# A decoder step on one core: copies of the sample caches moved from the state update to the down projection

## Chip, cores and metric

One core of one Trainium2 chip runs the whole kernel in one launch. The metric is the device time of that launch in microseconds (us).

## What is computed

The reference runs one layer of a hybrid decoder on a prompt of 512 tokens and on 8 sample tokens (one token for each of 8 sequences), width 1024, everything in float32. What matters here:

```python
# GLA, sample side: a state S of 4 heads x 128 x 256 per sequence (0.5 MB) is read, updated and written back
S = S * exp(blast) + k^T v ;  o = q @ S
# sliding-window attention, sample side: three caches per sequence (128, 512 and 1024 positions of 1024 floats);
# the new caches are the old ones shifted by one position, with the new key and value at the end
new_buf = stack([kall, vall])[:, kall.shape[1] - Lb:]
# attention scores get a relative bias looked up by distance; then branch projections, the output projection,
# and a gated FFN:
y = (silu(a_conv) * b) @ w_down
x = x + gate2 * y_f ;  out = rmsnorm(x)
```

The shift of a cache is nothing but a copy from DRAM to DRAM of all positions but the first: 508 KB for each of the 8 caches of group 1, 2044 KB for each of the 8 of group 2, and 4092 KB for each of the 8 of group 3. Nothing in the kernel reads these copies.

## The kernel before, in words

**Tiling.** The 520 token columns (512 + 8) stand on the free axis in two halves of 260, the features on the partitions. Every large matrix product is done in three passes (high part times high part, low part of the activations, low part of the weights), so a block of 128 x 128 weights costs six matmuls (`three_pass`, line 361). Weights come in units of 1 MB (`stream`), each unit being two output tiles of 8 blocks; a unit goes through three steps: SP's queue loads it into one of two slots of `wraw` (`issue`, `load`, line 318), ScalarE rounds it into `whi` (`split_hi`, line 332), VectorE subtracts to get `wlo` (`split_lo`, line 345). A slot of `wraw` is free for the next load once VectorE has finished its split.

**Stages.** In program order: an opening with the modulation vectors and the first norm; the GLA input units; the stage "gla" (11 units: the projections of attention group 0 and some gates are multiplied while the GLA recurrence runs between them); "att0" (9 units), "att1" (6) and "att2" (4), in which the attention of one group runs between the units of the next; the branch and output projections; the FFN's up projection (a loop over 22 units); and the down projection (8 output tiles `m`, each of two halves of 11 blocks with a load of 704 KB each). Then comes the final norm and the store of y.

**Order inside a streamed stage.** `stream_pe`, `stream_act` and `stream_dve` walk the stage's units. A `Between` object spreads the steps of the side work (generators such as `gla_pe`, `attention_pe`) evenly over four places in each unit. So each engine has one fixed order in which pieces of the unit's matmuls and steps of the side work alternate, and a side step that waits holds up the unit's matmuls behind it.

**The side work of "gla".** It has 41 steps over the 44 places of its 11 units: four heads of the prompt's recurrence, then two steps of preparation, then the 8 sample states (from about 0.75 of the stage on), then two steps that finish. For each sample state GpSimd's queue loads the state (line 1047) and a copy of the sample's value row broadcast over 128 partitions (line 1049), 512 KB each, into a ring of four slots; ScalarE scales the values by k (line 936), VectorE updates the state (line 1011), TensorE reads it out with q (line 883), and GpSimd stores it (line 1057, 512 KB). The first four loads are issued together. After that GpSimd waits, for each load, until the store of the state that was in the slot has landed and has been read out.

**The side work at the start of "att0".** GpSimd loads the table `onehot` (line 1160), VectorE waits for it (line 1196), TensorE makes the bias by distance (lines 1173 and 1175), VectorE evacuates it (line 1201), GpSimd writes it to DRAM (line 1162) and reads it back in a skewed form into `hank` (three DMAs, line 1167), and TensorE flips it (line 1185). SP's queue stores the GLA output, 2080 KB (line 1503), in the same stretch.

**The cache copies.** `moves` is a list of 33 copies in a fixed order: the small `conv_s` one, 8 of group 1 (508 KB), 8 of group 2 (2044 KB), 16 of group 3 (half a cache each, 2046 KB). Each call of `move_cache` (line 287) issues the next one on ScalarE's queue. `stream_act` calls it at the start of each of the 30 units of the four streamed stages, and the down projection calls it before each `split_hi`, 16 calls of which only the first three still find a copy. ScalarE waits for all copies at the very end, after its last instruction for y.

Of the kernel before, what the change touches and what calls it, by code (L numbers as in the profile page):

```python
# [139 lines left out]
def program(nc, w, o, con):  # L140
    U = stream(w)
# [22 lines left out]
    with ctx:  # L164
# [67 lines left out]
        def s(name):  # L232

            if name not in S:
                S[name] = sem(name)
            return S[name]
# [37 lines left out]
        for g in range(NG):  # L274
            pieces = 2 if g == 2 else 1
            for b in range(NS):
# [3 lines left out]
                for i in range(pieces):  # L280
                    r = slice(P // pieces * i, P // pieces * (i + 1))
                    moves.append((dst[r], src[r]))
        n_moved = [0]

        def move_cache(act):
            if n_moved[0] < len(moves):
                act.dma_start(*moves[n_moved[0]]).then_inc(caches_moved, 16)
                n_moved[0] += 1
# [161 lines left out]

        def stream_act(act, us, dst, work, steps, fine=False):
            between = Between(work, steps, us, fine)
            for u in us:
                move_cache(act)
                copy_tiles(act, u, dst, U[u]["m0"], between)
            between.finish()

# [80 lines left out]
        def square_act(act, i, k, X, tmp):  # L538
            if k >= 2:
                act.wait_ge(s("sq_added"), (KD - 1) * i + max(1, k - 2))  # L540
            act.activation(tmp["sq"][:, k % 2, :], X[:, k, :], ACT.Square).then_inc(s("sq_ready"), 1)
# [208 lines left out]
        def phase(name):  # L750
            return [u for u, x in enumerate(U) if x.get("phase") == name]
# [741 lines left out]
        for g in range(NG - 1):  # L1493
            with nc.Block() as block:
                us, here, there = phase(f"att{g}"), AQKV[g], AQKV[1 - g]
# [191 lines left out]
        with nc.Block() as block:  # L1687
            g_last = NG - 1
            us, here = phase("att2"), AQKV[g_last % 2]
# [45 lines left out]
            @block.scalar  # L1735
            def _(act):
                stream_act(act, us, None, attention_act(act, g_last, join_act(act)), n_steps, fine=True)
# [214 lines left out]
        with nc.Block() as block:  # L1952
# [36 lines left out]
            def _(act):  # L1989
# [22 lines left out]
                        unit(i, d, False)  # L2012
                for m in range(KD):
                    for half in range(2):
                        move_cache(act)
                        split_hi(act, vd0 + 2 * m + half + 1)
                    if m >= 1:
                        act.wait_ge(s("x_new"), KD + m)
                        if m == 1:
                            act.wait_ge(s("stored0"), CONV0 + 32 * (KF // 2))  # L2020
                            act.wait_ge(s("stored1"), CONV0 + 32 * (KF // 2))
                        square_act(act, 2, m - 1, xT, n3)
# [265 lines left out]
```

## Time and profile before

| | us |
|---|---|
| median of 3 runs | 1387.3 (1383.27 to 1394.7) |
| the profiled execution, its own time | 1388.96 |
| its span, first to last instruction | 1387.3 |
| mean granted TensorE clock in it | 0.945 of full speed |

Outside the span lie 1.7 us of the profiled execution. TensorE is busy for 91% of the span. A granted clock of 1.00 is 2.4 GHz, one of 0.50 is 1.2 GHz, and a number between them over a stretch is a mean of the two. TensorE's busy time in a stretch can therefore be high while it does half the work. Queue 0 in the DMA rows is GpSimd's, queue 1 is SP's, queue 10 is ScalarE's, that is the cache copies'.

### The profile page before, as it was taken

How to read it: one execution, taken by the hardware profiler on the slowest of the kernel's cores; microseconds unless marked ns; L12 is line 12 of the kernel's file. 1: busy time of each engine (PE TensorE's matmuls, PEld its weight loads, DVE VectorE, ACT ScalarE, POOL GpSimd, SP SyncE). 2: the span in 40 equal slices, each digit the busy share in tenths (PEclk: the TensorE clock that was granted, in tenths of full speed). 3: DMA queues.
4: the chain of work that ended last, by engine and by line, in shares of the span. 5: the costliest groups of instructions: out<-in, count | busy, mean ns of one | idle time of the engine just before them, and what ended most of it. 6: DMA issues, size and time to landing. Idle time of an engine off the chain costs nothing. (4 is left out here: it accounts for less than half of the span.)

```text
span 1387.3 us, 23268 instructions
## 1 busy us (share of the span) xinstructions
PE 1256.2 (91%) x9753; PEld 1159.8 (84%) x9753; DVE 611.1 (44%) x958; ACT 484.8 (35%) x770; POOL 107.0 (8%) x193
## 2 busy tenths in 40 slices
PE   5599999999679999999988689997899999999997
PEld 3479998888567998888776568997799999999996
DVE  0633134445331334343444836555766565652332
ACT  1573233344342443244242215333533333321212
POOL 1000000001211000020122011100000000010000
PEclk9589999999898999999989779999899999999998
DMA  7635543233986746666655647843333333346221
GB/s 230 198 122 173 162 127 103 88 110 122 369 321 247 245 152 224 217 229 218 224 183 199 245 139 267 283 152 91 92 92 91 90 90 89 86 131 198 84 83 61
DMA packets 165377, 229.84 MB, mean 166 GB/s; under 512 B 7316, under 2 KB 147982, under 8 KB 163868
## 3 DMA queue, kind: packets, MB, share of 16 engines
q1 hardware_dynamic: 148532, 123.76, 28.8%
q10 hardware_dynamic: 1424, 54.52, 10.8%
q0 software_dynamic: 15344, 50.45, 10.5%
q8 instruction: 59, 0.97, 0.3%
q14 instruction: 18, 0.15, 0.0%
HBM read 202.96 MB, written 80.26 MB: 204 GB/s over the span
## 5 line engine op out<-in xcount | busy, mean ns | idle before, releaser
L361 PE MATMUL ps<-actH,whi 128*128 128x260 f32 x2064 | 449.0, 300 | 25.0 <-DVE actL L573 17.8
L361 PE MATMUL ps<-actL,whi 128*128 128x260 f32 x2064 | 425.8, 289 | 0.0
L361 PE MATMUL ps<-actH,wlo 128*128 128x260 f32 x2064 | 425.4, 289 | 0.0
L361 PEld LDWEIGHTS ps<-actH,whi 128*128 128x128 f32 x2064 | 328.9, 196 | 68.1 <-issue 54.9
L361 PEld LDWEIGHTS ps<-actL,whi 128*128 128x128 f32 x2064 | 329.4, 195 | 0.0
L361 PEld LDWEIGHTS ps<-actH,wlo 128*128 128x128 f32 x2064 | 328.3, 195 | 0.0
L345 DVE TENSOR_TENSOR wlo<-wraw,whi 128x512 fp32r<-128x512 f32 (+3 forms) x95 | 141.1, 1498 | 188.5 <-ACT whi L332 187.8
L332 ACT ACTIVATE whi<-wraw 128x512 fp32r<-128x512 f32 (+3 forms) x95 | 119.6, 1275 | 135.9 <-PE ps L361 80.7
L410 ACT ACTIVATE arena<-ps 128x520 f32<-128x520 f32 x76 | 45.4, 600 | 219.3 <-PE ps L361 219.2
L361 PE MATMUL ps<-gH,whi 128*128 128x260 f32 x352 | 71.7, 285 | 0.0
L361 PE MATMUL ps<-gH,wlo 128*128 128x260 f32 x352 | 71.5, 285 | 0.0
L361 PE MATMUL ps<-gL,whi 128*128 128x260 f32 x352 | 71.4, 285 | 0.0
L1399 ACT ACTIVATE arena<-arena 128x128 f32<-128x128 f32 (+1 forms) x96 | 39.9, 417 | 54.0 <-DVE arena L1376 54.0
L2050 DVE TENSOR_TENSOR wlo<-wraw,whi 128x2048 fp32r<-128x2048 f32 x22 | 50.4, 2293 | 18.0 <-ACT whi L1995 18.0
L361 PEld LDWEIGHTS ps<-gL,whi 128*128 128x128 f32 x352 | 54.9, 190 | 0.0
L361 PEld LDWEIGHTS ps<-gH,wlo 128*128 128x128 f32 x352 | 54.9, 191 | 0.0
L361 PEld LDWEIGHTS ps<-gH,whi 128*128 128x128 f32 x352 | 54.8, 190 | 0.0
L515 DVE COPY arena<-ps 128x256 f32<-128x256 f32 x24 | 10.1, 422 | 77.8 <-PE ps L496 77.8
L1995 ACT ACTIVATE whi<-wraw 128x2048 fp32r<-128x2048 f32 x22 | 41.8, 1901 | 0.0
L1370 DVE SCALAR_TENSOR_TENSOR arena<-ps,arena 128x512 f32<-128x512 f32 (+1 forms) x32 | 20.9, 653 | 39.7 <-PE ps L1321 39.7
L496 PE MATMUL ps<-wraw,scP 128*32 128x256 f32 x384 | 31.1, 451 | 5.7 <-DMA wraw<-in_w_ada 5.7
L1977 POOL DMA_DIRECT2D out_conv_p<-arena x22 | 11.3, 514 | 323.5 <-DVE arena L2091 217.9
(306 smaller groups left out, 1456.7 us busy)
## 6 DMA issues: line engine op xcount, KB each, us to landing
wraw<-in_w_in SPq DMA_DIRECT2D x38, 1024.0 KB, 5.4
out_win_s<-in_cache_win ACTq DMA_DIRECT2D x16, 2046.0 KB
wraw<-in_w_ada SPq DMA_DIRECT2D x24, 1024.0 KB, 5.5
wraw<-in_w_up SPq DMA_DIRECT2D x44, 512.0 KB, 5.0
out_win_s<-in_cache_win ACTq DMA_DIRECT2D x8, 2044.0 KB
raw_gates<-arena SPq DMA_DIRECT2D x24, 260.0 KB, 6.0
arena<-raw_gates POOLq DMA_DIRECT2D x24, 260.0 KB, 4.5
wraw<-in_w_down SPq DMA_DIRECT2D x16, 384.0 KB, 3.3
```

The source lines that it names most:

```text
L332: ins = act.activation(whi[:, v % 2, c], wraw[:, u % 2, c], ACT.Copy)
L345: ins = dve.tensor_tensor(wlo[:, v % 2, c], wraw[:, u % 2, c], whi[:, v % 2, c].bitcast(F32), ALU.subtract)
L361: last = pe.matmul(ps[:, 2 * (n % 2) + a, 0:HT], wt, X[:, k0 + j, a * HT:a * HT + HT], start=begin and j == 0 and wt is hi and X is H, sto ...
L410: act.activation(halves(to), banks(n), ACT.Copy).then_inc(tile_read["act"], 1)
L496: last = pe.matmul(ps[QC * j:QC * j + QC, 7, 0:2 * P], scP[:, k, :], wraw[:, u % 2, 2 * k * P:2 * (k + 1) * P], start=half == 0, stop=half ...
L515: dve.tensor_copy(rows[:, a % 2, :], ps[:, 7, 0:2 * P]).then_inc(ada_tok, 1)
L1370: dve.scalar_tensor_tensor(sv, ps[:, 4 + n % 2, 0:nh * J].rearrange("p (h k) -> p h k", k=J), SCALE, biasT[:, hs, lo:hi], ALU.mult, ALU.ad ...
L1399: last = act.activation(sv, sv, ACT.Exp, bias=bnd[:, c % 2, b0 + AE:b0 + AE + 1], accum_out=bnd[:, c % 2, b0 + AE + 1:b0 + AE + 2])
L1977: pool.dma_start(o["conv_p"][:, col], ast[0:2, store.slot, :]).then_inc(s(f"stored{store.slot}"), 16)
L1995: act.activation(whi[:, vn % 2, :], wraw[:, (up0 + 1 + d) % 2, :], ACT.Copy).then_inc(hi_ready, 1)
L2050: dve.tensor_tensor(wlo[:, vn % 2, :], wraw[:, (up0 + 1 + d) % 2, :], whi[:, vn % 2, :].bitcast(F32), ALU.subtract).then_inc(lo_ready, 1)
```

## The change

`stream_act` calls `move_cache` only in the first six of the eleven units of the stage "gla" (`M_GLA = 6`); in the other stages it calls it in every unit, as before. The down projection calls it once for each output tile `m` instead of twice. The order of the list stays as it is, so every later copy moves back by five calls:

| stage | copies before | copies after |
|---|---|---|
| gla | conv, 8 of group 1, 2 of group 2 | conv, 5 of group 1 |
| att0 | 6 of group 2, 3 of group 3 | 3 of group 1, 6 of group 2 |
| att1 | 6 of group 3 | 2 of group 2, 4 of group 3 |
| att2 | 4 of group 3 | 4 of group 3 |
| down projection | 3 of group 3 | 8 of group 3 |

```diff
@@ -281,6 +281,7 @@
         n_moved = [0]
+        M_GLA = 6
 
         def move_cache(act):
@@ -450,8 +451,9 @@
             between = Between(work, steps, us, fine)
-            for u in us:
-                move_cache(act)
+            for j, u in enumerate(us):
+                if U[u]["phase"] != "gla" or j < M_GLA:
+                    move_cache(act)
                 copy_tiles(act, u, dst, U[u]["m0"], between)
             between.finish()
@@ -2012,7 +2014,8 @@
                 for m in range(KD):
                     for half in range(2):
-                        move_cache(act)
+                        if half == 0:
+                            move_cache(act)
                         split_hi(act, vd0 + 2 * m + half + 1)
```

## Rows read from the trace of the kernel before

**Rows 1.** The page: TensorE's busy time; queue 10, packets, MB, share.
```profile
PE 1256.2 (91%) x9753; PEld 1159.8 (84%) x9753; DVE 611.1 (44%) x958; ACT 484.8 (35%) x770; POOL 107.0 (8%) x193
...
q10 hardware_dynamic: 1424, 54.52, 10.8%
```

**Rows 2.** DMA issues of the whole span: the small copies.
```profile
out_win_s<-in_cache_win ACTq DMA_DIRECT2D x8, 508.0 KB
```

**Rows 3.** Busy time in stretches of 5 us, 370 to 440 us.
```profile
core 0: us, PE busy (x) PEld busy (x) DVE busy (x) ACT busy (x) POOL busy (x), PEclk, DMA share, GB/s
...
370.00:375.00 5.00, 0.99 (x9) 0.78 (x7) 0.00 (x0) 0.00 (x0) 2.04 (x3) 1.00 1.01 360
...
380.00:385.00 5.00, 5.00 (x26) 4.80 (x23) 1.67 (x4) 1.71 (x4) 1.93 (x4) 0.50 0.99 362
...
415.00:420.00 5.00, 5.00 (x16) 2.23 (x17) 2.19 (x4) 0.00 (x0) 0.60 (x1) 0.60 1.03 435
420.00:425.00 5.00, 5.00 (x34) 5.00 (x33) 0.00 (x0) 0.60 (x1) 2.71 (x3) 0.72 0.28 68
...
435.00:440.00 5.00, 3.54 (x11) 2.51 (x12) 0.00 (x0) 0.60 (x1) 0.00 (x0) 0.66 0.81 284
```

**Rows 4.** Groups of instructions by line, 345 to 405 us.
```profile
L883 PE MATMUL ps<-arena 128*32 128x256 f32 x64 | 5.6, 425 | 12.5 <-DVE arena L1011 12.5
```

**Rows 5.** DMA queues, 345 to 405 us: packets, MB, share.
```profile
q0 software_dynamic: 3456, 12.58, 57.8%
q10 hardware_dynamic: 96, 4.19, 19.1%
```

**Rows 6.** Timeline of ScalarE: start, us, what, [idle before it].
```profile
359.40 0.52 ACTq L287 DMA_DIRECT2D out_win_s<-in_cache_win  x1
...
375.73 1.70 ACT L936 ACTIVATE arena<-arena 128x256 f32<-128x256 f32 x4 [8.10 <-DMA arena<-sample_values]
...
403.86 0.53 ACTq L287 DMA_DIRECT2D out_win_s<-in_cache_win  x1
...
427.41 0.52 ACTq L287 DMA_DIRECT2D out_win_s<-in_cache_win  x1
```

**Rows 7.** Timeline of GpSimd, 364 to 405 us.
```profile
364.72 0.76 POOL L1047 DMA_DIRECT2D arena<-in_state_gla  x1 [4.50 <-DMA out_gla_s<-arena]
...
404.89 0.55 POOL L1160 DMA_DIRECT2D arena<-in_onehot  x1
```

**Rows 8.** Timeline of TensorE, 379 to 415 us.
```profile
379.19 1.08 PE L883 MATMUL ps<-arena 128*32 128x256 f32 x8 [8.20 <-DVE arena L1011]
...
414.19 0.80 PE L1173 MATMUL ps<-arena 33*8 33x384 f32 x2 [3.26 <-DVE arena L1196]
```

**Rows 9.** Who waited for whom, 404 to 440 us.
```profile
PE ps L1185 <- DMA arena<-bias_by_distance: 2.9, 1, 2.9
```

**Rows 10.** DMA issues, 1240 to 1265 us: KB, median to landing.
```profile
out_win_s<-in_cache_win ACTq DMA_DIRECT2D x3, 2046.0 KB
...
wraw<-in_w_down SPq DMA_DIRECT2D x2, 320.0 KB, 15.1
```

**Rows 11.** Timeline of ScalarE in the down projection.
```profile
1263.66 1.38 ACT L332 ACTIVATE whi<-wraw 128x1408 fp32r<-128x1408 f32 x1 [10.83 <-DMA wraw<-in_w_down]
...
1299.00 1.38 ACT L332 ACTIVATE whi<-wraw 128x1408 fp32r<-128x1408 f32 x1 [6.53 <-PE ps L361]
...
1347.85 0.62 ACT L541 ACTIVATE arena<-arena 128x520 f32<-128x520 f32 x1
```

**Rows 12.** Timeline of VectorE in the down projection.
```profile
1284.56 1.63 DVE L345 TENSOR_TENSOR wlo<-wraw,whi 128x1408 fp32r<-128x1408 f32 x1 [6.18 <-ACT whi L332]
```

**Rows 13.** Timeline of the loads' and outputs' queue (SP), 1243 us on.
```profile
1243.81 99.72 SPq L318 DMA_DIRECT2D wraw<-in_w_down  x26
...
1382.91 1.04 SPq L1969 DMA_DIRECT2D out_y_sample<-arena  x1
```

**Rows 14.** The chain that ended last: start, us, what.
```profile
1241.80 128.46 PE ps L361 x1056
```

## The prediction

> **What bounds the kernel now.** I read the page's busy times first: TensorE is busy for 91% of the span, no other engine for half of it [rows 1]. So time is only to be won where TensorE idles or runs at its lower clock, and the question is whether a copy stands behind such a place. The busy time in stretches of 5 us shows where those places are: between 370 and 375 us TensorE works for 0.99 us, and from 380 to 385 us it is "busy" for all 5 us with a granted clock of 0.50, the lower level, so it does half the work; the same pair, a gap and then a lower clock, stands around 410 to 425 us and around 435 us [rows 3]. The groups of instructions say that in the sample states TensorE idled 12.5 us before the read-outs (line 883) [rows 4], and the timeline that 8.20 us of it are one wait, for the fifth state [rows 8]. ScalarE began that state at 375.73 after 8.10 us of waiting for a DMA, the broadcast value row [rows 6]. Then I looked at what the DMA engines did there.
>
> **What a copy costs the others.** ScalarE's queue kept 16 engines busy for 10.8% of 1387.3 us, which is 149.8 us, for 54.52 MB [rows 1]: 2.75 us a MB. A copy of 2046 KB (2.10 MB) is 5.8 us of all engines, one of 508 KB (0.52 MB) [rows 2] is 1.4 us. In the sample states queue 0 moved 12.58 MB in 3456 packets, 3.6 KB each, and the copies 4.19 MB in 96, 44 KB each; together with SP's queue they filled the engines [rows 5], with a DMA share of 0.99 and 1.01 [rows 3]. A copy of this kind, once started, is thus a block that small packets of another queue stand behind.
>
> **Term 1, the sample states.** Five copies leave the stage: three of 508 KB, before the states are loaded, where nothing waits for a DMA (I count them at nothing), and two of 2044 KB. The first of these two was issued at 359.40 [rows 6], while GpSimd waited 4.50 us for a store to land, so that it could issue the fifth load at 364.72 [rows 7]. That load landed 11 us later (375.73), against the 5.8 us by which the copy fits in between. Without the copy the load comes at least 5.8 us sooner, and the store before it a little sooner as well. What is late then: TensorE reaches the read-out at 379.19 - 8.20 = 371.0 and would still wait one or two us, and the later states go by the pace of their own DMAs, 12.58 MB at 57.8% of the engines. So the whole is pulled forward by the shift of the DMAs, not by all that TensorE lost. Bounds: 0 (the states' own 12.6 MB set the pace in any case) and 8.2 + 2.5 = 10.7 (the whole gap, and (1 - 0.50) x 5 us of lower clock). I take 6.5. The second copy, at the end of the states, has no wait of TensorE's behind it: 0.
>
> **Term 2, the table of the bias.** The first copy of "att0" was issued at 403.86 [rows 6], the table `onehot` at 404.89 [rows 7]; TensorE waited 3.26 us for what VectorE makes of it, until 414.19 [rows 8]. That copy becomes one of 508 KB, 4.4 us shorter, so the table lands 4.4 us sooner and the gap of 3.3 us goes; next is TensorE itself. The lower clock behind the gap cost (1 - 0.60) x 5 + (1 - 0.72) x 5 = 3.4 us [rows 3]. Part of that stretch is small matmuls which wait for each other through VectorE, so I count on two thirds of it. Bounds 0 and 6.7; I take 3.3 + 2.2 = 5.5.
>
> At this place a rule of the Trainium skill speaks against the change. The page "DMA: Bandwidth & Descriptors", section "Issuing engines are not separate DMA queues", says that DMAs from different engines run on the same 16 DMA engines and interleave. If they shared evenly, the table's 0.2 MB would have landed early in spite of the copy, its wait would have another cause, and term 2 would be 0, the sum 9.5. The packet sizes of rows 5 speak for the block instead.
>
> **Term 3, the flipped bias.** The second copy of "att0" (427.41) [rows 6] ran into the three loads of the skewed bias, and TensorE waited 2.9 us for them [rows 9], with (1 - 0.66) x 5 = 1.7 us of lower clock after it [rows 3]. This copy too shrinks by 4.4 us. But TensorE now comes to the place sooner, by the 2.2 us of clock of term 2, so 2.9 - 4.4 + 2.2 = 0.7 us of the wait stay. Gain 2.2, and 0.8 of the clock: 3.0. Bounds 0 and 4.6. The third copy shrinks too, and nothing waits there: 0. From the fourth unit of "att0" to the end of "att2" every call issues about the same 2.1 MB as before: 0.
>
> **Term 4, the down projection.** It gets eight copies in place of three. TensorE's chain runs through it without a break: 128.46 us for 16 halves, 8.03 us each [rows 14]. What a half's weights may cost: VectorE ends a split at 1284.56 + 1.63 = 1286.2 [rows 12], then SP loads the half that ScalarE rounds at 1299.00 [rows 11], 12.8 us later. The two splits take 1.38 and 1.63 us and TensorE needs the result a half after 1299.00, so 8.0 - 3.0 = 5 us are left over: a load may take 17.8 us. In the first tile, where three copies stood in 12 us, one load took from 1243.81 [rows 13] to 1263.66, 19.8 us, and ScalarE waited 10.83 us for it [rows 11], and even then TensorE's chain is one piece [rows 14]. The median of the two 320 KB loads there was 15.1 us [rows 10]. With one copy per tile (16 us) a load has at most 5.8 us in front of it. So the stage costs 0, between 0 and 25 (below); a gain is excluded, since nothing there waits now. The issue itself, 0.52 us on ScalarE [rows 6], lies in idle time of over 6 us [rows 11]. The last copy is issued behind the square at 1347.85 [rows 11], about 34 us before the last output's DMA at 1382.91 [rows 13]; it needs 5.8. Cost at the end: 0.
>
> **Sum.** 6.5 + 5.5 + 3.0 = 15.0 us. The profiled execution took 1388.96 us, so 1374.0 after. The median of the runs is 1.7 us lower, and the forecast goes by it: 1387.3 - 15.0 = 1372.3, said as 1372.
>
> **Rivals.** (a) *Only part of it.* The states' own DMAs fill the engines, so the time saved on the copy is waited for again at the next state, and only the two waits in "att0" go: 5.5 + 3.0 = 8.5 us, 1379; or the reverse, term 1 alone with 6.5, 1381. For it: DMA share near 1.0 even in 370 to 375 us, where no copy ran [rows 3]. Against it: a load that took 11 us with 5.8 us of copy in it. Chance 0.27, at 1380. (b) *All waits and their lower clock go*: 10.7 + 6.7 + 4.6 = 22 us, 1365. For it: each low clock stands behind a gap. Chance 0.15. (c) *Slower.* The down projection's loads come too late behind their copies. It decides at 17.8 us from issue to landing. At the 19.8 us seen once, 2.0 us would be missing in each of seven tiles, and a gap of that size brings some 1.5 us of lower clock (the 8.2 us gap brought over 2.5): 7 x 3.5 = 25 us. With the three terms gained this is 1397, without them 1412. Against it: it takes a load to stand behind two or more copies, and there is one in 16 us. Chance 0.05. (d) *The copies were hidden and nothing moves*: other DMAs take the same room; 1387. Chance 0.03.
>
> **How the numbers follow.** The forecast holds 0.50, with 1368 to 1376 as its own range (11 to 19 us). A measurement of this kernel can tell some 1% from no change, which is 13.9 us, or 1373.4. Two thirds of the forecast's range lie below that. Faster by over 1%: 0.50 x 0.66 + 0.15 = 0.48. Within 1%: 0.17 + 0.27 + 0.03, and half of (c) with 0.02, so 0.49. Slower by over 1%: the rest of (c), 0.03. The range, 1364 to 1384, takes in (a), (b) and the forecast, and leaves out (c), (d) and the outer ends.
>
> **What would show it.** In the changed profile: the wait of TensorE before the read-outs falls from 12.5 to about 6 us; ScalarE's longest wait for the value row from 8.1 to under 3; `onehot` lands in under 6 us from its issue, and no wait stands before line 1173; the wait before line 1185 is under 1 us; granted clocks near 1.00 where 0.50, 0.60, 0.72 and 0.66 stood; queue 10 absent between the sixth unit of "gla" and "att0"; the down projection's chain again 128 to 129 us, with eight copies beside it and ScalarE waiting for no load. The forecast is wrong if the sample states last as long as before with queue 10 silent, if new waits for a DMA stand in "att0", or if the down projection's chain is cut.

## The result, and the profile after

The changed kernel took 1380.3 us (median of 20 runs, 1374.84 to 1388.68), the kernel before, on the same chip, 1391.5 us (20 runs, 1382.77 to 1395.83). The ratio is 0.9937, interval 0.9919 to 0.9954: 0.6% faster, some 8.8 us. The forecast had 15.0 us, 1.1%. The direction was right; the gain is little more than half of it. Measured a second time, beside 35 runs of the kernel before, the ratio was 0.9959 (0.9930 to 0.9989), 5.7 us. The two intervals reach from 6.4 to 11.3 us and from 1.5 to 9.7 us.

The profiled execution took 1376.58 us (span 1374.9), 12.4 us less than the one of before. Not all of that is the change's: the opening, up to ScalarE's first pass over the norm, took 59.8 us in the one and 55.8 in the other, although nothing is changed there, and over all the profiles of this study, changed or not, it took 54.4 to 60.8. These 4.0 us are scatter. The stretch from the middle of "att2" to the down projection scatters too, 472.5 and 472.0 us before and 470.5 and 472.0 after in two profiles each, and I compare pieces of the span from here on.

Lines of the changed kernel stand one to three further down: L883 is L885, L936 is L938, L1173 is L1175, L1185 is L1187, L361 is L362.

The page of the kernel after: TensorE is busy 9.0 us less, and queue 10 has the same packets and megabytes as in [rows 1]. Nothing was saved, only moved.
```profile
PE 1247.2 (91%) x9753; PEld 1152.7 (84%) x9753; DVE 611.2 (44%) x958; ACT 484.9 (35%) x770; POOL 107.4 (8%) x193
...
q10 hardware_dynamic: 1424, 54.52, 11.0%
```

The sample states after. First the timeline of ScalarE at the eight states (start, us, what, [idle before it]), the rows that answer to the second one of [rows 6]:
```profile
346.15 1.70 ACT L938 ACTIVATE arena<-arena 128x256 f32<-128x256 f32 x4 [2.06 <-DMA arena<-sample_values]
352.02 1.71 ACT L938 ACTIVATE arena<-arena 128x256 f32<-128x256 f32 x4 [4.16 <-DMA arena<-sample_values]
356.71 1.70 ACT L938 ACTIVATE arena<-arena 128x256 f32<-128x256 f32 x4
360.12 1.69 ACT L938 ACTIVATE arena<-arena 128x256 f32<-128x256 f32 x4
366.14 1.71 ACT L938 ACTIVATE arena<-arena 128x256 f32<-128x256 f32 x4 [1.62 <-DMA arena<-sample_values]
372.12 1.71 ACT L938 ACTIVATE arena<-arena 128x256 f32<-128x256 f32 x4 [4.27 <-DMA arena<-sample_values]
377.96 1.70 ACT L938 ACTIVATE arena<-arena 128x256 f32<-128x256 f32 x4 [3.64 <-DMA arena<-sample_values]
```
And the same timeline of the kernel before: its first state, and its fourth to eighth without the fifth, which stands in [rows 6] (375.73, 8.10 us of waiting).
```profile
350.54 1.71 ACT L936 ACTIVATE arena<-arena 128x256 f32<-128x256 f32 x4 [1.00 <-DMA arena<-sample_values]
...
363.23 1.70 ACT L936 ACTIVATE arena<-arena 128x256 f32<-128x256 f32 x4
...
380.84 1.71 ACT L936 ACTIVATE arena<-arena 128x256 f32<-128x256 f32 x4 [3.41 <-DMA arena<-sample_values]
386.13 1.70 ACT L936 ACTIVATE arena<-arena 128x256 f32<-128x256 f32 x4
390.81 1.71 ACT L936 ACTIVATE arena<-arena 128x256 f32<-128x256 f32 x4 [1.18 <-DMA arena<-sample_values]
```
The fifth state comes 6.0 us after the fourth instead of 12.5: that is the forecast of term 1, exactly. But the sixth, seventh and eighth follow at 6.0, 5.8 and 5.9 us, where they followed at 5.1, 5.3 and 4.7. From the first state to the fourth it is 1.3 us longer too. From the first to the eighth it is 37.75 us (the last starts at 383.90) against 40.27, so of the 6.5 us 4.0 are given back.

The waits of TensorE after, in the whole span (us in total, times, longest), the line that answers to [rows 4] and the longest wait of [rows 8]; then the one that answers to [rows 9]:
```profile
PE ps L885 <- DVE arena L1013: 11.2, 7, 3.7
...
PE ps L1187 <- DMA arena<-bias_by_distance: 4.3, 1, 4.3
```
Six waits with a longest of 8.2 us have become seven with 3.7 at most, and the sum has hardly moved (12.5 before). The wait before the flip has grown, from 2.9 to 4.3. The wait before line 1175 is gone (3.26 us in [rows 8]).

DMA queues after, in the stage of the states (341 to 396 us), for [rows 5]: queue 10 is absent, and queue 0 now takes 64.2% of the engines for the same 12.58 MB (in 55 us instead of 60).
```profile
q0 software_dynamic: 3456, 12.58, 64.2%
```

Stretches of 5 us after, for [rows 3]:
```profile
core 0: us, PE busy (x) PEld busy (x) DVE busy (x) ACT busy (x) POOL busy (x), PEclk, DMA share, GB/s
...
345.00:350.00 5.00, 1.30 (x12) 0.96 (x15) 1.67 (x4) 1.70 (x4) 0.08 (x1) 0.91 1.01 343
350.00:355.00 5.00, 5.00 (x28) 4.31 (x21) 1.25 (x4) 1.71 (x4) 0.69 (x1) 0.50 1.05 368
355.00:360.00 5.00, 4.81 (x38) 4.04 (x37) 1.98 (x6) 3.79 (x6) 1.03 (x2) 0.91 0.88 332
360.00:365.00 5.00, 4.53 (x42) 3.50 (x43) 3.99 (x6) 2.42 (x6) 3.65 (x6) 1.00 0.73 220
365.00:370.00 5.00, 3.27 (x32) 2.83 (x31) 1.67 (x4) 1.71 (x4) 1.62 (x4) 1.00 1.01 346
370.00:375.00 5.00, 3.32 (x32) 2.93 (x24) 1.13 (x3) 2.20 (x5) 1.54 (x3) 1.00 1.04 389
375.00:380.00 5.00, 4.41 (x27) 4.00 (x28) 0.84 (x3) 2.04 (x5) 1.12 (x2) 0.66 1.05 401
...
405.00:410.00 5.00, 5.00 (x22) 3.25 (x21) 1.91 (x4) 0.00 (x0) 0.61 (x1) 0.71 1.03 362
...
425.00:430.00 5.00, 3.80 (x11) 2.77 (x12) 0.00 (x0) 0.60 (x1) 0.00 (x0) 0.50 0.65 241
```
Three things are to be seen. The DMA share is 1.01 to 1.05 in 345 to 355 and again in 365 to 380, with no copy there, so the states' own transfers and SP's fill the engines; in 355 to 365 it falls to 0.88 and 0.73. TensorE, which did 0.99 us of work in 370 to 375 before, does 3.3 us in each of 365 to 370 and 370 to 375, at a granted clock of 1.00. And stretches at or towards the lower level remain: 350 to 355, behind the gap of 345 to 350; 375 to 380 (0.66); 405 to 410 (0.71), where TensorE has been busy without a gap since 400; 425 to 430, behind the wait before the flip.

The down projection after: the chain that ended last, and the DMA issues of 1232 to 1365 us (KB, median us to landing), for [rows 14] and [rows 10].
```profile
1230.98 126.94 PE ps L362 x1056
```
```profile
out_win_s<-in_cache_win ACTq DMA_DIRECT2D x7, 2046.0 KB
wraw<-in_w_down SPq DMA_DIRECT2D x13, 384.0 KB, 6.7
wraw<-in_w_down SPq DMA_DIRECT2D x13, 320.0 KB, 7.3
```
One piece of 126.94 us with the copies beside it. With one copy in 16 us the loads land in about 7 us, less than half of the 15.1 of [rows 10].

### The profile page after: what moved, and what is told of

Read it like the earlier page. It is cut to its first block and busy times, and to the rows that moved or that the text cites. A ratio compares the mean times of both kernels' runs of the same rounds, so it can differ in the third digit from the quotient of the medians.

```text
span 1374.9 us, 23268 instructions
## 1 busy us (share of the span) xinstructions
PE 1247.2 (91%) x9753; PEld 1152.7 (84%) x9753; DVE 611.2 (44%) x958; ACT 484.9 (35%) x770; POOL 107.4 (8%) x193
## 3 DMA queue, kind: packets, MB, share of 16 engines
q10 hardware_dynamic: 1424, 54.52, 11.0%
## 5 line engine op out<-in xcount | busy, mean ns | idle before, releaser
L362 PE MATMUL ps<-actH,whi 128*128 128x260 f32 x2064 | 446.7, 298 | 26.9 <-DVE actL L575 20.4
L362 PE MATMUL ps<-actH,wlo 128*128 128x260 f32 x2064 | 423.8, 288 | 0.0
L362 PE MATMUL ps<-actL,whi 128*128 128x260 f32 x2064 | 423.8, 288 | 0.0
L362 PEld LDWEIGHTS ps<-actH,whi 128*128 128x128 f32 x2064 | 327.1, 194 | 70.4 <-issue 55.1
L362 PEld LDWEIGHTS ps<-actL,whi 128*128 128x128 f32 x2064 | 327.5, 194 | 0.0
L362 PEld LDWEIGHTS ps<-actH,wlo 128*128 128x128 f32 x2064 | 326.8, 194 | 0.0
L362 PE MATMUL ps<-gH,whi 128*128 128x260 f32 x352 | 71.1, 283 | 0.0
L362 PE MATMUL ps<-gH,wlo 128*128 128x260 f32 x352 | 70.8, 282 | 0.0
L362 PE MATMUL ps<-gL,whi 128*128 128x260 f32 x352 | 70.7, 282 | 0.0
L362 PEld LDWEIGHTS ps<-gL,whi 128*128 128x128 f32 x352 | 54.3, 188 | 0.0
L362 PEld LDWEIGHTS ps<-gH,whi 128*128 128x128 f32 x352 | 54.2, 188 | 0.0
L362 PEld LDWEIGHTS ps<-gH,wlo 128*128 128x128 f32 x352 | 54.2, 188 | 0.0
L2004 ACT ACTIVATE arena<-arena 128x520 f32<-128x520 f32 x22 | 14.1, 641 | 63.7 <-DVE arena L2070 63.7
```

The costliest lines, as they stand in the source:

```text
L362: last = pe.matmul(ps[:, 2 * (n % 2) + a, 0:HT], wt, X[:, k0 + j, a * HT:a * HT + HT], start=begin and j == 0 and wt is hi and X is H, sto ...
L2004: act.activation(sg5, acc, ACT.Sigmoid).then_inc(s("ffn_sig"), 1)
```

## The experiments

Each kernel was measured beside the kernel before on the same chip, 3 to 5 rounds, where nothing else is said. The differences between the variants, 0.1 to 0.4%, mostly lie inside their intervals, so the verdicts rest on pieces of the span: from the start of ScalarE's work on the first state to that on the eighth (*states*), from the evacuation of the last "gla" tile to that behind the bias table (*table*), from there to the evacuation of the first flip (*flip*), and from ScalarE's second split in the down projection to its last instruction (*end*). Each is worked out from two starts in the timeline of ScalarE. The landings are those of the DMA issues, the waits TensorE's.

| kernel | ratio | states | table | flip | end | `onehot` lands in | wait before 1175 | wait before 1187 |
|---|---|---|---|---|---|---|---|---|
| before | 1 | 40.3 | 21.1 | 14.6 | 130.3 | 8.7 | 3.3 | 2.9 |
| before, again | | 40.1 | 21.0 | 16.8 | 133.0 | 8.5 | 3.1 | 5.1 |
| after | 0.9937 | 37.7 | 16.3 | 16.0 | 130.3 | 4.2 | none | 4.3 |
| after, again | 0.9959 | 37.6 | 14.8 | 17.1 | 130.3 | 4.2 | none | 5.4 |
| e1 | 0.9969 | 38.3 | 22.6 | 10.4 | 129.5 | 8.6 | 3.2 | none |
| e2 | 0.9977 | 39.5 | 16.3 | 14.1 | 129.5 | 3.1 | none | 2.5 |
| e3 | 0.9990 | 37.5 | 16.3 | 13.7 | 139.7 | 2.9 | none | 2.6 |
| e4 | 0.9960 | 37.1 | 23.1 | 10.4 | 130.3 | 9.3 | 3.9 | none |
| e5 | 0.9939 | 35.8 | 14.8 | 17.1 | 129.5 | 4.6 | none | 5.4 |
| e6 | 1.0022 | 37.3 | 14.8 | 17.1 | 136.7 | 4.0 | none | 5.4 |
| e7 | 0.9948 | 37.5 | 16.3 | 13.5 | 130.3 | 3.3 | none | 2.4 |
| e8 | 0.9958 | 37.9 | 14.8 | 17.3 | 129.5 | 3.3 | none | 5.6 |
| e11 | 1.0019 | 40.1 | 17.3 | 17.1 | 133.0 | 6.4 | 1.0 | 5.4 |
| e12 | 0.9916 | 37.7 | 14.8 | 17.2 | 130.3 | 4.0 | none | 5.6 |

**The two kernels again.** The changed kernel unchanged:

> The changed kernel once more, unchanged, to learn which pieces of its profile repeat. My theory now (from the two profiles: sample states 2.7 us shorter from the first to the last, bias table 4.8 us sooner, the wait for the skewed bias longer, not shorter): the same pieces come again within 0.5 us each, the sum being some 8 to 10 us against the kernel before (ratio 0.993 to 0.9945). Rival (scatter): the pieces come and go with the execution; then the states or the table differ by over 2 us from the first profile of the changed kernel, and the ratio may lie anywhere from 0.990 to 0.998. The opening, up to the first norm, was 4.0 us shorter in the profile of the changed kernel although nothing in it was changed: I expect it to vary by several us either way.

and, later, one more profile of the kernel before:

> The kernel before once more, one look, to learn how far its own pieces repeat. Theory: sample states 40 us from the first to the eighth as before (the four kernels without copies beside them had 37.5, 37.6, 37.5 and 38.2), a wait of 3 us before line 1173, onehot landing 8.6 us after its issue; the wait before the flip (line 1185) may be anywhere from 0 to 3 us, since the kernel with the same copies at that place (only the states' copies withheld) had none. Rival (the first profile was an odd one): the states take under 38.5 us.

Both show how far one profile may be trusted: the states repeat within 0.2 us and the table within 1.5, the wait before the flip does not (2.9 and 5.1 before, 4.3 and 5.4 after). The 2.9 us on which term 3 was built were one draw. So was the unbroken chain of the down projection: in the second profile of the kernel before it goes through a load of the weights, and the stage's *end* is 2.7 us longer (133.0 against 130.3).
```profile
1248.18 19.93 DMA wraw<-in_w_down
...
1271.29 103.33 PE ps L361 x858
```
e11 below, with the copies of the kernel before in other rows, has it too (a load of 19.77 us, 133.0).

**e1, no copies beside the states, the head of "att0" as it was** (it still has copies of 2044 KB):
```diff
-        M_GLA = 6
+        M_GLA = 9
```


> M_GLA = 9: only the two copies of 2044 KB beside the sample states are withheld, the small ones stay where they were before, so that att0 begins with copies of 2.1 MB as before; the down projection gets 5. Theory (the copy is a block, the states go by the pace of their own bytes): fifth state 6 us sooner against the fourth, pitch of the later ones 5.9 us instead of 5.0, so 2.5 to 3 us in all for the stage; the table onehot lands 8 to 9 us after its issue again and TensorE waits some 3 us before line 1173; ratio 0.997 to 0.999. Rival 1 (my prediction's term 1): the stage gains 6.5 us, ratio 0.995. Rival 2 (the small copies before the states matter too): less than 1 us gained here.

0.9969 (0.9942 to 0.9997). The states gain 1.9 us of the 2.5 that they gain in the changed kernel (38.3 against a mean of 40.2), and `onehot` lands in 8.6 us with its wait of 3.2 us, as before. So the wait before line 1175 belongs to the copy at that place and is not a consequence of the states. But the flip then waits for nothing and comes after 10.4 us, and table and flip together take 33.1 us with the copies of the kernel before, whose own two profiles have 35.7 and 37.8. Against this run the changed kernel (32.3 and 31.8) gains only 1.0 us at the place, against the kernel before 4.6. The gain of the table is shown; how large that of both pieces together is, is not.

**e2, only the first two copies of "att0" gone, the states as before:**
```diff
-                if U[u]["phase"] != "gla" or j < M_GLA:
+                if U[u]["phase"] != "att0" or j >= 2:
```


> All copies of the gla stage stay as before, the first two units of att0 issue none, the down projection issues one per tile and gets 5. Theory: the states as before (no gain), the table onehot lands in under 4 us and TensorE waits nothing before line 1173, 4.8 us gained up to there as in the changed kernel or a little more; the wait before the flip (line 1187 of the changed kernel) stays at 3 to 5 us although no copy stands in its way, because the write of the bias runs into the GLA output's store and the skewed loads into a weight load; ratio 0.995 to 0.997. Rival (the small copy behind the skewed loads makes that wait): it falls to under 1 us, ratio 0.993 to 0.995.

0.9977 (0.9950 to 1.0004). The waits of this kernel in the sample states:
```profile
PE ps L885 <- DVE arena L1013: 12.5, 7, 8.0
```
The 8.0 us wait is back, the table's is gone. The two causes are separate. The ratios, 0.31% and 0.23% against 0.63% and 0.41% for both, go with a plain sum, but their intervals reach 0.3% to either side, and this run's takes in no change.

**e3, neither of them, and no copy in the first three units of "att0"; eleven copies in the down projection, two in each of its first three tiles:**
```diff
-                if U[u]["phase"] != "gla" or j < M_GLA:
+                if j < M_GLA if U[u]["phase"] == "gla" else U[u]["phase"] != "att0" or j >= 3:
...
-                        if half == 0:
+                        if half == 0 or m < 3:
```


> The changed kernel, with no copy in the first three units of att0 either; the down projection gets 11, two in each of the first three tiles. Theory: against the changed kernel at most 1 us more from the table, and the wait before the flip falls only by what the 1.4 us copy takes, from 4.3 to about 3; the down projection's chain stays whole at 128 to 129 us with loads that take up to 20 us; ratio 0.991 to 0.994. Rival (the copy makes the wait): the wait before the flip is under 1 us, 4 us more gained. Rival (down projection breaks): its chain is over 131 us.

0.9990 (0.9962 to 1.0017). The places it was meant for gain (table and flip together 30.0 us, against 32.3 and 31.8 after), and the down projection loses 9.4 us. Its part of the chain that ended last:
```profile
1233.31 20.34 DMA wraw<-in_w_down
1253.68 1.39 ACT whi L333
...
1257.51 14.67 DMA wraw<-in_w_down
...
1275.95 14.39 DMA wraw<-in_w_down
...
1293.45 73.14 PE ps L362 x594
```
The chain no longer is TensorE's for the first 62 us; it goes from load to load.

**e4, SP's 2080 KB store of the GLA output issued before the stream of "att0" instead of behind its first unit:**
```diff
-                    stream_sp(sp, us[:1])
...
-                    stream_sp(sp, us[1:])
+                    stream_sp(sp, us)
```


> The changed kernel, with the GLA output's store (2080 KB) issued at the start of att0, ahead of the first weight load of the stage instead of behind it. Theory (the little write of the bias stands behind that store, and so the skewed loads come late): the write lands in 3 us instead of 5.1, and TensorE's wait before the flip (line 1187) falls from 4.3 and 5.4 us to between 2 and 3.5; the table onehot may land 1 to 2 us later, since the store now runs beside it, still without a wait of over 1 us before line 1175. Rival (the remaining small copy makes the wait): it stays above 4 us. Time against the changed kernel: 1 to 3 us less, under what the comparison can tell.

0.9960 (0.9948 to 0.9973), no other than the changed kernel. The wait moved: `onehot` now stands beside the store and lands in 9.3 us (3.9 us of waiting before line 1175), the bias write behind it lands in 2.3 us and the flip waits for nothing. Table and flip together 33.5 us, 1.4 more than in the changed kernel. Moving the 2 MB moved the wait and saved nothing.

**e5, 1.57 MB less for the last four states** (of the broadcast value row only the first head's part is loaded; the sample output of the other heads is left to what lies in the buffer):
```diff
-                    pool.dma_start(vwide[:, d, :], vd[b:b + 1, :].to_broadcast([P, D])).then_inc(slot_in("gs", d), 16)
+                    n = D if b < SD else GDV
+                    pool.dma_start(vwide[:, d, 0:n], vd[b:b + 1, 0:n].to_broadcast([P, n])).then_inc(slot_in("gs", d), 16)
```


> The changed kernel, with the value row of the last four sample states loaded only for the first head (128 KB instead of 512 KB each), so 1.57 MB less beside the states; the other heads of these four states use what stands in the buffer, so part of the output differs. Theory (after the change the states go by the pace of their own bytes): the pitch of the fifth to eighth state falls from 5.9 us to about 4.3, TensorE's own pace there being 4.1, and the eighth comes 4 us sooner (1.57 MB at 2.75 us a MB is 4.3). Rival (the pace is the latency of store, wait, load through the ring of four): pitch stays over 5.3 us, under 2 us gained.

The states took 35.8 us, 1.9 less than in the changed kernel (mean 37.65). By bytes alone it should have been 4.3, by latency alone close to nothing. Inconclusive between the two: both have a part.

**e6, two copies per tile in the down projection, eight in its first four tiles:**
```diff
-                        if half == 0:
-                            move_cache(act)
+                        move_cache(act)
```


> The changed kernel, but the down projection issues before every split again, so its eight copies stand in the first four tiles, two in each. Theory (from the run with eleven copies, whose chain was cut three times and grew by 9 us): loads of the weights take 20 us and more, TensorE's chain is cut two or three times and the stage is 5 to 9 us longer; ratio to the changed kernel 1.004 to 1.006. Rival (the eleven, not the two per tile, made it): the chain stays whole at 128 to 129 us.

1.0022 (1.0009 to 1.0036): the whole gain is lost, and a little more. Waits in the down projection, 1232 to 1365 us, of any engine:
```profile
ACT whi L333 <- DMA wraw<-in_w_down: 38.4, 5, 14.0
```
and the chain that ended last:
```profile
1258.26 14.42 DMA wraw<-in_w_down
...
1276.46 14.15 DMA wraw<-in_w_down
...
1293.72 73.14 PE ps L362 x594
```
The second edit of the change, one copy per tile, is thus what makes the first one pay: end 136.7 us against 130.3.

**e7, the copies of "att0"'s first two units moved to two units of "gla" before the states are loaded:**
```diff
-        M_GLA = 6
+        M_GLA = 8
...
-                if U[u]["phase"] != "gla" or j < M_GLA:
+                if j < M_GLA if U[u]["phase"] == "gla" else U[u]["phase"] != "att0" or j >= 2:
```


> The copies of the first two units of att0 are moved into the seventh and eighth unit of the gla stage (small ones, before the states are loaded); the down projection has eight, one per tile, as in the changed kernel. Theory: small copies before the states cost nothing (states as in the changed kernel within 0.5 us), onehot lands in 3 us, the wait before the flip is 2.5 us as in the two runs without copies there; 1.5 to 2.5 us less up to the flip than the changed kernel, nothing lost in the down projection. Rival (copies in the seventh and eighth unit delay the first states): the first state comes over 1 us later.

0.9948 (0.9930 to 0.9967). Table and flip together 29.8 us, 2.3 less than in the changed kernel; the wait before the flip falls to 2.4. The small 508 KB copies at this place are not free: the three kernels without them (e2, e3, e7) have 29.8 to 30.4 us there, the five with them (after twice, e5, e6, e12) 31.8 to 32.3. The ratio doesn't tell it from the changed kernel. One reason may be the rival of this run: from ScalarE's first pass over the norm to its first state it took 292.3 us, against 290.4 and 291.2 in the changed kernel (291.6 in e8, which has the same two copies there), so the copies before the states may cost a microsecond. One profile each doesn't settle it.

**e8, e7 with the store of the GLA output held back until the bias write has landed:**
```diff
+                        sp.wait_ge(s("bias_spilled"), 16)
```


> The kernel with the copies of the first two units of att0 moved into the seventh and eighth unit of gla, and with the GLA output's store issued once the write of the bias has landed. Theory: the write lands in 2.4 us instead of 5.1; the skewed loads then run beside the store, so half of that is given back; up to the flip 0 to 2 us less than the 29.8 us of the kernel without this. Rival: the store, on which ScalarE waits ahead of the first flip, is now what comes last, 1 to 3 us more. Time under what a comparison can tell.

0.9958 (0.9938 to 0.9978). The write lands in 2.3 us instead of 5.1, as meant, but the store now runs into the three loads of the skewed bias, which take 11.6 to 13.7 us, and the flip waits 5.6 us. Worse than e7 by 2.3 us there. It shows the same as e4 from the other side: the store only changes what it is in the way of.

**e9 and e10, the same copies in short rows**, on the kernel before and on the changed one: 508, 2044 and 4092 bytes a row instead of packets of some 38 KB (54.52 MB in 1424, [rows 1]).
```diff
-                src = w[f"cache_win{g + 1}"][b].rearrange("t n -> (t n)")[D:WIN[g] * D].rearrange("(p n) -> p n", n=n)
-                dst = o[f"win{g + 1}_s"][b].rearrange("t n -> (t n)")[0:(WIN[g] - 1) * D].rearrange("(p n) -> p n", n=n)
+                src = w[f"cache_win{g + 1}"][b].rearrange("t n -> (t n)")[D:WIN[g] * D].rearrange("(a p n) -> p a n", p=P, n=WIN[g] - 1)
+                dst = o[f"win{g + 1}_s"][b].rearrange("t n -> (t n)")[0:(WIN[g] - 1) * D].rearrange("(a p n) -> p a n", p=P, n=WIN[g] - 1)
```


> The kernel before, all copies at their old places, but each copy is written as rows of 508 to 4092 bytes that don't adjoin, in place of pieces of 64 KB; bytes and count of DMAs the same. Theory (a copy hurts because its packets are long and the short ones of other queues stand behind them): onehot lands 3 to 5 us after its issue in spite of a copy of 2044 KB one us ahead of it, the 3 us wait before line 1173 is gone; in the sample states the fifth state is less late (under 10 us after the fourth instead of 12.5), the whole of the states 38 to 40 us. Rival (it is the bytes alone): onehot lands in 8 us as before and the wait stays. The small rows may make the copies themselves slower, up to twice the engines' time.

> The changed kernel with the same short rows. Theory: the states and the table as in the changed kernel, within 1 us, since no long packet stood there; the down projection's loads, which take 7 us beside a copy now, take 4 to 7 us. Time the same as the changed kernel's within what can be told. Rival (short rows make the copies so slow that the down projection's loads come too late): its chain is cut, over 131 us.

1.0974 and 1.0833: 9.7% and 8.3% slower than the kernel before. The edit did more than cut the packets; it made the copy itself slow. DMA packets and queues of e9 between 365 and 377 us:
```profile
DMA packets 511, 1.05 MB, mean 88 GB/s; under 512 B 7, under 2 KB 501, under 8 KB 511
...
q10 hardware_dynamic: 494, 1.01, 106.9%
q0 software_dynamic: 17, 0.04, 3.4%
```
1.01 MB of queue 10 filled all engines for 12 us (the rows here were 2044 bytes long), and queue 0 got 17 packets in that time. So these runs don't test the length of a packet at an equal rate. They do show that short packets of a slow copy hold the others too: the fifth state came 32.8 us after the fourth, `onehot` landed in 26.3 us and TensorE waited 19.4 us for it. In e10 states and table have no copy or only small ones beside them and stay at 37.6 and 16.4 us, while the time from the first flip to the evacuation of the new tokens in the second unit of "att1" is 268.0 us instead of 165.8 and 164.5.

**e11 and e12, the same copies in aligned rows of 4096 bytes**, one position of a cache each (and a second small DMA for what is left of 16):
```diff
+                    strided = lambda v: v[0:k, :].rearrange("(a p) n -> p a n", p=16)
+                    parts = [(strided(d_), strided(s_))]
```


> The kernel before, each copy written as whole positions of 4096 bytes whose neighbours go to the same DMA 16 positions apart (plus a small DMA of up to 15 positions for the rest), so packets of 4 KB in place of 64 KB, and aligned, unlike the rows of 508 to 4092 bytes. Theory A (a DRAM to DRAM copy holds the engines for as long as it lasts, whatever its packets; the short rows were bad because they made it last 25 us): if the copy keeps its rate, onehot lands in 8 to 9 us as before and TensorE's wait before line 1173 stays near 3 us. Theory B (long packets block, and the misaligned rows were bad for another reason): onehot lands in under 5 us and the wait is gone; the fifth state comes under 10 us after the fourth. If the copy is slow again, the time is over 1420 us and the two are not told apart by the table, but queue 0's bytes during the copy tell: A has next to none.

> The changed kernel with the same 4 KB rows. Theory A: within 1% of the changed kernel if the copies keep their rate, its down projection's loads at 7 us as now. Theory B: loads at 4 to 5 us in the down projection. If the copies are slow: both over the changed kernel, and att1 and att2 carry most of it.

Here the cost is kept: the page of e11 gives queue 10 ten times the packets and almost the share of [rows 1].
```profile
q10 hardware_dynamic: 14224, 54.52, 11.2%
```
e11 measured 1.0019 (0.9995 to 1.0043), no change. During the copy that stands beside the states, 363 to 368 us, the queues of e11:
```profile
q10 hardware_dynamic: 322, 1.32, 70.5%
q0 software_dynamic: 166, 0.59, 29.4%
```
and the same view of the second profile of the kernel before, where the copy has its long packets:
```profile
q10 hardware_dynamic: 30, 1.31, 67.5%
q0 software_dynamic: 69, 0.26, 14.8%
```
The copy moves the same 1.3 MB, and queue 0 moves 0.59 MB beside it instead of 0.26. These 5 us lie later in the one copy than in the other, though (issued at 358.99 in the second profile, at 359.99 in e11). In 363 to 365, where both run in full, the long packets move 0.92 MB of copy beside 0.05 MB of queue 0, the short ones 0.51 beside 0.27. So the block is real, and short packets soften it, at the price of a copy that lasts longer: `onehot` lands in 6.4 us instead of 8.5, its wait is 1.0 instead of 3.1. Over the whole copy, 359 to 372 us, nothing is won: queue 0 moves 2.44 MB in e11 and 2.54 and 2.03 in the two profiles of the kernel before, and the states take 40.1 us as before. There it was the copy's bytes that counted.

e12 had the best time of all, 1375.55 us, 0.9916 (0.9888 to 0.9944). Its interval overlaps the changed kernel's, and states, table and flip are those of the changed kernel's second profile to 0.2 us. What is shorter is the opening (54.4 us, which scatters) and the stretch from the evacuation of the new tokens in the second unit of "att1" to just behind "att2", 220.8 us against 222.6 and 223.5 (220.7 in e11, 223.2 and 224.4 before). But e2 has 220.9 there with the long packets. I don't claim it as better; whether short aligned rows are worth 2 us there stays open.

## Why the prediction was right or wrong

**What bounds the kernel: right.** The time came from the places with a gap of TensorE and a lower clock behind it. What other stretches gained or lost is no more than their scatter, except in the down projection (term 4).

**Term 1, sample states, 6.5 forecast, 2.5 measured** (a mean of 40.2 to 37.65, two profiles each): this is the step that failed. The prediction said that "the whole is pulled forward by the shift of the DMAs". The shift is there, 6.5 us at the fifth state, but it isn't kept to the eighth: the three states after it come at 5.9 us a piece instead of 5.0, which gives 2.7 us back, and 1.3 were lost ahead of it; in the second profile 4.6 us were gained at the fifth and 2.0 given back. Rival (a) had named this, and its row stood in [rows 3]: a DMA share of 1.01 in 370 to 375 us, where no copy ran. I read that row as evidence for the rival and then priced the term by the latency of one load.

That price rested on a wrong reading too, "a load that took 11 us with 5.8 us of copy in it". DMA queues of the kernel before from the issue of the fifth load to its landing, 364.7 to 375.7 us:
```profile
q0 software_dynamic: 628, 2.32, 56.7%
q1 hardware_dynamic: 630, 0.65, 17.9%
q10 hardware_dynamic: 27, 0.72, 17.3%
```
1.37 MB of the copy had been moved by 364.7, and the 0.72 MB that were left are 2.0 us at 2.75 us a MB; from 367.5 us on it moved nothing. The rest of the 11 us went to queue 0 itself, which had moved only 0.07 MB in 363 to 367, and to SP's queue.

Without the copy the engines have less to do, but the stage does not shorten by as much. Their share over the states is 1.04 of 40.5 us before (350.5 to 391), 42.1 us, and 0.96 of 38 us after (346 to 384), 36.5 us: 5.6 us less work, 2.5 us less time. (A share above 1 shows that the records overlap somewhat; the sums are estimates.) After, the engines are short of work in 355 to 365 (shares of 0.88 and 0.73), where GpSimd waits 3.25 us for a store before it issues the fifth load at 359.74. From 365 on they are full, and the loads behind the fifth are slow: from issue to the start of ScalarE's work the seventh and eighth took 10.2 and 9.8 us (367.72 to 377.96, 374.07 to 383.90), before 8.5 and 8.1 (377.62 to 386.13, 382.73 to 390.81). So the bytes and the ring of four slots both have a part. GpSimd waits for a slot's store before it issues the next load, 15.8 us in all before and 9.3 after, as the groups of the kernel after show:
```profile
L1049 POOL DMA_DIRECT2D arena<-in_state_gla x7 | 5.3, 755 | 9.3 <-DMA out_gla_s<-arena 9.3
```
e5 bears it out: 1.57 MB fewer gave 1.9 us, neither 4.3 nor nothing. How the two share the rest was not separated, nor was which of the two copies beside the states, at 359.40 or at 386.12, cost what.

The clock that was to be won back at 380 to 385 us came back there, and some of it went again at 375 to 380 (0.66), where TensorE waited 2.27 us for the sixth state.

**Term 2, the table, 5.5 forecast, 5.5 measured** (21.05 to a mean of 15.55). `onehot` lands in 4.2 us, the wait is gone, and of the lower clock behind it part remains (0.71 in 405 to 410 us, with TensorE busy since 400), as the two thirds assumed. e1 and e2 show the cause at that place from both sides, and e11, where the copy stays and only its packets are short, already has 17.3 us. That the size came out to the tenth is luck: the two profiles after have 16.3 and 14.8. On the rule of the Trainium skill that was weighed there ("DMA: Bandwidth & Descriptors", "Issuing engines are not separate DMA queues"): the DMAs of different queues do interleave, as 69 packets of queue 0 beside 30 of queue 10 in 5 us show, and the trace agrees so far, but not to equal bytes. Read as equal shares, the rule would have made term 2 0; the traces say 5.5.

**Term 3, the flipped bias, +3.0 forecast, about −0.9 measured** (a mean of 15.7 to 16.55). The gain of 3.0 did not come. Whether the place lost anything isn't shown: it took 14.6 and 16.8 us before, 16.0 and 17.1 after, and 10.4 in e1, which has the copies of the kernel before there. The step that failed is "2.9 - 4.4 + 2.2 = 0.7 us of the wait stay": it counts only the three loads that TensorE names as its releaser. Before them in the same chain stands GpSimd's write of the bias to DRAM (line 1164), and it too can be late. GpSimd after, then before (its second row is the issue of the three loads, with the wait for the write in brackets):
```profile
407.85 0.61 POOL L1164 DMA_DIRECT2D bias_by_distance<-arena  x1 [9.30 <-DVE arena L1203]
413.56 2.71 POOL L1169 DMA_DIRECT2D arena<-bias_by_distance  x3 [5.11 <-DMA bias_by_distance<-arena]
```
```profile
418.96 0.60 POOL L1162 DMA_DIRECT2D bias_by_distance<-arena  x1 [13.52 <-DVE arena L1201]
422.29 2.71 POOL L1167 DMA_DIRECT2D arena<-bias_by_distance  x3 [2.73 <-DMA bias_by_distance<-arena]
```
Before, the write was issued at 418.96, about 3 us before the end of SP's store of the GLA output (issued at 409.21, landed 12.6 us later), and from 420 on it met free engines (DMA share 0.28 in 420 to 425) [rows 3]. After, term 2's success brings it to 407.85, still 5.6 us before the end of that store (issued at 402.32, landed 11.1 us later), at a DMA share of 1.03, and 36 KB take 5.4 us instead of 3.0 (5.5 and 3.1 in the second profiles).
```profile
402.32 0.57 SPq L1505 DMA_DIRECT2D gla_out<-arena  x1
```
A chain brought forward ran into a transfer of which it used to meet only the end. e4 and e8 shift that store to either side and show the collision: the write then lands in 2.3 us. Neither wins, as the 2 MB then stand before the table or before the loads. And e7 shows that the 508 KB copies left at this place cost 2.3 us of the 32.1; the forecast had taken them for harmless.

**Term 4, the down projection, 0 forecast, 0 or 2.7 measured.** After, the chain is in one piece and ScalarE waits for no load, as forecast. That "a gain is excluded, since nothing there waits now" was wrong: the three copies in a row of the kernel before stand at the edge. A load of 19.8 us left the chain whole in its first profile, one of 19.93 us cut it in the second, and there the change gains 2.7 us, in the mean 1.3. The condition of rival (c), two copies in front of a load, was right: in e6 the chain goes through three loads and 6.4 us are lost. Its threshold of 17.8 us was too high for loads in a row: behind a first one of 18.97 us two of 14.42 and 14.15 us stand on the chain as well. Its price of 25 us was four times too high: over the last nine halves the chain is in one piece again (73.14 us), in e6 with hardly a copy beside them, in e3 with one per tile.

**The sum.** 2.5 + 5.5 − 0.9 + 1.3 = 8.4 us by pieces, against 8.8 and 5.7 us by the two ratios; the two pieces at the head of "att0", 4.6 together, are the least certain (1.0 against e1). Of the forecast's 15.0 us, 4.0 were lost at the states and 3.9 at the flip. The time lay inside the range, near rival (a)'s 1380. Its mechanism for the states was right for the greater part, but that its number came so near is luck: it gave the states nothing and "att0" 8.5 us, and they brought 2.5 and 4.6.

**The marks to look for.** Right: `onehot` under 6 us, no wait before line 1175, queue 10 absent, the down chain whole with eight copies (126.94 us). Wrong: the wait before the read-outs 11.2 and not 6, ScalarE's longest wait 4.27 and not under 3, the wait before line 1187 4.3 and not under 1, clocks of 0.66 and 0.71 and 0.50 still there.

## What to carry to other kernels

A load that a copy delayed by 6 us gave 2.5 us back here, because others came behind it: where the stage's other transfers keep the engines at a share of 1.0, or a ring makes each load wait for a store, read the whole stage from first to last and not the longest wait, and ask the queue's own bytes how much of the copy was still in front of the load when it was issued. Where a fix brings a chain forward, list every DMA of that chain, also the small ones that no row names as a releaser, and look what runs at the time to which they move. Bulk copies belong beside a stage whose loads have slack, spread evenly: at one per 16 us they were free, at two they took back the whole gain. And take a second profile before a term of 3 us is built on one wait.

## What the runs showed of the hardware

- DRAM to DRAM copies depend strongly on the shape of their rows. With 1424 packets, 38 KB each in the mean, 54.52 MB took 10.8% of the engines for 1387.3 us; with aligned rows of 4096 bytes 11.2% of 1386.4; with rows of 508, 2044 and 4092 bytes, not aligned, 18.5% of 1523.9. Of these the 2044 byte rows were seen by themselves: 1.01 MB in 106.9% of 12 us is 12.7 us a MB, against 2.75. Why was not tried.
- What a queue gets beside a copy depends on the size of the copy's packets: in 363 to 365 us, 0.05 MB beside 0.92 MB of copy in long packets (44 KB in the mean), 0.27 MB beside 0.51 MB in 4 KB ones. Over the whole copy (13 us) it got 2.03 to 2.54 MB either way.
- The granted clock also fell without a gap: 0.71 in 405 to 410 us after, where TensorE is busy for all 5.00 us, as it is from 400 to 405, and from 404 to 407 at small matmuls of the bias. The wait removed here didn't bring back all of the clock behind it.
- The opening of this kernel scatters by 6.4 us from one execution to the next, over two fifths of the 15.0 us forecast; the pieces above repeat within 0.2 to 2.7 us.
